# Two middle MLP groups of a decoder layer: pairs of units, with seven products of block sums in two of eight steps

## What is computed

```python
v = rms_norm(h, g_mlp[i])
h = h + jnp.square(jax.nn.relu(v @ w_mlp_up[i])) @ w_mlp_down[i]
h = h + jax.nn.sigmoid(h @ w_ple_gate[i]) * (p[i] @ w_ple_proj[i])
```

## Time and profile before

| | |
|---|---|
| median of three runs | 1570.44 us (1570.18 to 1570.52) |
| the profiled execution | 1570.37 us, of which the span of the profile is 1568.6 us |
| granted clock of TensorE | 0.998 of full speed |
| PE, DVE, ACT, POOL busy | 1560.0, 1073.4, 925.5, 147.8 us |
| MLP groups 1 and 2 | from 951 us of the span, 174 us each |

### The profile page before, as it was taken

How to read it: one execution, slowest core, us unless ns; L and a number is a source line. 1 busy time by engine, 2 the same in 40 slices (tenths; PEclk the granted TensorE clock), 3 DMA queues, 4 the chain that set the end, 5 groups by cost and what they waited for, 6 DMA issues and landing times.

```text
span 1568.6 us, 19800 instructions
## 1 busy us (share of the span) xinstructions
PE 1560.0 (99%) x7186; PEld 1287.6 (82%) x7186; DVE 1073.4 (68%) x1287; ACT 925.5 (59%) x1372; POOL 147.8 (9%) x247
## 2 busy tenths in 40 slices
PE   9999999999999999999999999999999999999998
PEld 8888887878878888888888888888888888888887
DVE  6679988768999958986655545565456555656665
ACT  6574466655454555767687544773467535777754
POOL 0222376443000000000000000000000000000000
PEclk9999999999999999999999999999999999999999
DMA  9766566656766668876656666666666666666663
GB/s 324 269 197 194 161 208 221 196 194 188 216 201 211 205 211 298 281 264 207 193 181 203 200 191 188 200 188 201 190 187 199 192 195 188 191 199 194 221 193 130
DMA packets 93764, 324.25 MB, mean 207 GB/s; under 512 B 10864, under 2 KB 14448, under 8 KB 93296
## 3 DMA queue, kind: packets, MB, share of 16 engines
q1 hardware_dynamic: 93536, 322.88, 66.0%
q10 hardware_dynamic: 144, 0.26, 0.1%
HBM read 312.62 MB, written 10.49 MB: 206 GB/s over the span
## 4 chain that ended last, share of the span: by engine, by line
PE 99%; ACT 0%; ACTq 0%; issue 0%; POOL 0%; DVE 0%; POOLq 0%
PE ps L427 32%; PE ps L429 31%; PE ps L428 31%; PE ps L731 0%; PE ps L734 0%; PE ps L988 0%; PE ps L987 0%; PE ps L989 0%; PE ps L737 0%; PE ps L815 0%; PE ps L840 0%; PE ps L891 0%; PE ps L715 0%; PE ps L902 0%; PE ps L802 0%; PE ps L746 0%
## 5 line engine op out<-in xcount | busy, mean ns | idle before, releaser
L410 DVE TENSOR_TENSOR sb<-sb,sb 128x1024 fp32r<-128x1024 f32 x552 | 676.8, 1231 | 407.6 <-ACT sb L403 402.3
L403 ACT ACTIVATE sb<-sb 128x1024 fp32r<-128x1024 f32 x552 | 581.9, 1057 | 522.2 <-PE ps L429 492.1
L427 PE MATMUL ps<-sb,sb 128*128 128x512 f32 (+1 forms) x2176 | 846.6, 389 | 0.0
L428 PE MATMUL ps<-sb,sb 128*128 128x512 f32 (+1 forms) x2176 | 843.8, 388 | 0.0
L429 PE MATMUL ps<-sb,sb 128*128 128x512 f32 (+1 forms) x2176 | 843.7, 388 | 0.0
L427 PEld LDWEIGHTS ps<-sb,sb 128*128 128x128 f32 x2176 | 408.4, 188 | 88.8 <-issue 4.2
L429 PEld LDWEIGHTS ps<-sb,sb 128*128 128x128 f32 x2176 | 408.4, 188 | 84.3
L428 PEld LDWEIGHTS ps<-sb,sb 128*128 128x128 f32 x2176 | 408.5, 188 | 83.1
L473 ACT ACTIVATE ps<-ps 32x256 f32<-32x256 f32 x464 | 162.8, 351 | 29.6 <-DVE ps L462 23.6
L1321 POOL TENSOR_TENSOR sb<-sb,sb 128x1 f32<-128x1 f32 x1 | 0.6, 560 | 1172.5 <-DVE sb L1990 1172.5
L499 POOL COPY sb<-sb 32x256 f32<-32x256 f32 (+1 forms) x112 | 76.0, 679 | 189.0 <-DVE sb L491 184.6
(11 more groups left out here) (238 smaller groups left out, 601.8 us busy)
## 6 DMA issues: line engine op xcount, KB each, us to landing
sb<-in_w_gate SPq DMA_DIRECT2D x128, 512.0 KB, 3.9
sb<-in_w_up SPq DMA_DIRECT2D x128, 512.0 KB, 3.9
sb<-in_w_down SPq DMA_DIRECT2D x128, 512.0 KB, 4.1
sb<-in_w_mix SPq DMA_DIRECT2D x56, 512.0 KB, 4.3
sb<-in_w_branch SPq DMA_DIRECT2D x32, 512.0 KB, 4.7
sb<-in_w_out SPq DMA_DIRECT2D x32, 512.0 KB, 3.8
sb<-in_w_pg SPq DMA_DIRECT2D x32, 512.0 KB, 4.0
gate_mem<-sb SPq DMA_DIRECT2D x16, 512.0 KB, 5.3
```

Source lines behind the costliest of these rows:

```text
L403: act.activation(whi[:, j % RING, :], raw[:, j % RING, :], ACT.Copy).then_inc(hi_done, 1)
L410: eng.tensor_tensor(wlo[:, j % RING, :], raw[:, j % RING, :], whi[:, j % RING, :].bitcast(F32), ALU.subtract).then_inc(lo_done, 1)
L427: pe.matmul(o, xh, w_h, start=first and k == 0, stop=False)
L428: pe.matmul(o, xh, w_l, start=False, stop=False)
```

## The change

Groups 1 and 2 leave `mlp_group` for a new body, four calls of `pair_of_units(g, p)` in each pass of the loop on each engine. A pair is two units (c = 0, 1) side by side, 16 tiles (i = 0 to 15). Steps j = 0 to 5 take unit 0's tile and then unit 1's tile of the same two k blocks; the last four tiles are (6, 0), (7, 0), (6, 1), (7, 1), so that unit 0 ends at tile 13 and unit 1 at tile 15. The pair's own sums lie in `acc` for an even pair and in `side` for an odd one.

In steps 2 and 5 (tiles 4 and 5, 10 and 11) the 2 x 2 x 2 block product of two token blocks, two k blocks and two units is made with seven products in place of eight. Three of the seven go into the pair's own banks and four into "temporaries", the banks of the other kind. For that DVE makes four sums of weight blocks (`t_raw`, in three operations) which ACT and DVE split into `t_high` and `t_low`, and `wlo` of the second tile is made only for its second half. The sums of token blocks (`up_raw`, `dn_raw`) are made once for v in group 0's seventh unit, and once a step for f in the second and third pair. At i = 12 ACT copies one temporary and DVE makes four linked sums of them into `extra` (the place of `t_raw`), which DVE adds to each unit's result. "Linked" means that DVE waits for the operation's own semaphore before the next.

The square of an up unit goes from DVE to ACT, behind the ReLU, which reads SBUF now (DVE has written main + extra there). Transposes go to SBUF (`pair_lane`), and of the sixteen block moves GpSimd makes eight and ACT eight. SP's loop covers groups 1 and 2 in the pair's order, and group 3's loads are written out.

```diff
+SEVEN = (2, 5)
+STEP_TILES = [2 * j for j in SEVEN]
+PAIR_ORDER = [(j, c) for j in range(TPU - 2) for c in range(2)] + [(j, c) for c in range(2) for j in (TPU - 2, TPU - 1)]
+UNIT_ENDS = [PAIR_ORDER.index((TPU - 1, c)) for c in range(2)]
+PAIR_STEPS = 48
...
+extra = at(t_at, [2, TT, CW])
+pair_lane = [scratch[:, 0, :], at(top, [TT * CW])]
...
+def pair_of_units(g, p):
+    up = p < PAIRS // 2
...
+    pe.wait_ge(temps_free, g * PAIRS + (p - PAIRS + 1))
+    if p == 0:
+        pe.wait_ge(grp_free, g * (4 * NCH) + (2 * G_FF - 2))
+    for i, (j, c) in enumerate(PAIR_ORDER):
+        u, jj = pair_tile(g, p, i)
...
+        if p == PAIRS // 2 and i in (0, TPU, TPU + TPU // 2):
+            pe.wait_ge(tp_lo, g * NCH + (TP_FF + {0: NCH - 2, TPU: NCH - 1}.get(i, NCH)))
...
+        if j in SEVEN:
+            if c:
+                continue
+            e = SEVEN.index(j)
+            if e == 0:
+                pe.wait_ge(grp_free, g * (4 * NCH) + (2 * G_FF + 4 * p))
...
+            pe.wait_ge(lo_done, u * TPU + (jj + 1))
+            three(temp_bank(p, 0), half(x_hi_, 0, 0), half(x_lo_, 0, 0), block(whi, s, 0), block(wlo, s, 0),
+                  first, last)
+            three(main_bank(p, 0, 0), half(x_hi_, 1, 0), half(x_lo_, 1, 0), block(whi, s, 1), block(wlo, s, 1),
+                  False, False).then_inc(tile_used, 1)
+            pe.wait_ge(lo_done, u * TPU + (jj + 2))
+            if up:
+                pe.wait_ge(up_sums_lo, len(SEVEN))
+            else:
+                pe.wait_ge(dn_sums_lo, g * len(SEVEN) + (e + 1 - len(SEVEN)))
+            three(main_bank(p, 1, 0), sh(4), sl(4), block(whi, s + 1, 1), block(wlo, s + 1, 1), False, False)\
+                .then_inc(tile_used, 1)
+            n = 2 * (len(SEVEN) * (p - PAIRS) + e)
+            pe.wait_ge(comb_lo, g * (2 * PAIRS * len(SEVEN)) + (n + 1))
+            three(temp_bank(p, 1), sh(1), sl(1), t_high[:, 0, :], t_low[:, 0, :], first, last)
+            three(temp_bank(p, 3), sh(3), sl(3), t_high[:, 1, :], t_low[:, 1, :], first, last)
+            pe.wait_ge(comb_lo, g * (2 * PAIRS * len(SEVEN)) + (n + 2))
+            three(temp_bank(p, 2), sh(2), sl(2), t_high[:, 2, :], t_low[:, 2, :], first, last)
+            three(main_bank(p, 0, 1), half(x_hi_, 1, 1), half(x_lo_, 1, 1), t_high[:, 3, :], t_low[:, 3, :],
+                  False, False).then_inc(seven_done, 1)
+            continue
...
             mlp_group(0, True, False)
             with pe.Fori(1, NFG - 1) as g:
-                mlp_group(g, False, False)
+    for p in range(PAIRS):
+        pair_of_units(g, p)
+pe.wait_ge(temps_free, (NFG - 2) * PAIRS + 1)
...
+def pair_of_units(g, p):
...
+    for i in range(2 * TPU):
+        u, jj = pair_tile(g, p, i)
+        t = i + AHEAD
+        if t - 1 in STEP_TILES:
+            e = STEP_TILES.index(t - 1)
+            s = (jj + AHEAD) % RING
+            act.wait_ge(raw_in[s], u * (16 * TPU // RING) + 16 * ((jj + AHEAD) // RING + 1))
+            act.wait_ge(tile_used, u * TPU + (jj + AHEAD - RING + 1))
+            act.activation(whi[:, s, C:2 * C], raw[:, s, C:2 * C], ACT.Copy).then_inc(hi_done, 1)
+            n = 2 * (len(SEVEN) * (p - PAIRS) + e)
+            if e:
+                act.wait_ge(seven_done, g * (PAIRS * len(SEVEN)) + (n // 2))
+            if p in (1, 2) and i == 2:
+                act_blocks(0, range(12, 16)).then_inc(tp_in, 1)
+            for b in range(2):
+                act.wait_ge(comb_raw, g * per + (n + b + 1))
+                act.activation(t_high[:, 2 * b:2 * b + 2, :], t_raw[:, 2 * b:2 * b + 2, :], ACT.Copy)\
+                    .then_inc(comb_hi, 1)
+        else:
+            split_hi(act, u, jj + AHEAD)
+        if i == 12:
+            act.wait_ge(seven_done, g * (PAIRS * len(SEVEN)) + len(SEVEN) * (p + 1 - PAIRS))
+            act.activation(extra[:, 0, 0, :], temp_bank(p, 0), ACT.Copy).then_inc(first_copied, 1)
+        def relu_square(c, q):
+            act.wait_ge(grp_free, g * (4 * NCH) + 2 * (G_FF + 2 * q + c + 1))
+            for tt in range(TT):
+                part = relu[c][:, tt * C:(tt + 1) * C]
+                ins = act.activation(part, part, ACT.Relu, scale=rstd[:, 1, tt:tt + 1])
+                ins.then_inc(relu_done, 1)
+            act.wait_ge(relu_done, g * (2 * NCH) + 2 * (2 * q + c + 1 - NCH))
+            act.activation(relu[c][:, :], relu[c][:, :], ACT.Square).then_inc(sg["sq_done"], 1)
+        if i == UNIT_ENDS[0] + 1 and p < 2:
+            relu_square(0, p)
+        if p in (1, 2):
+            n = 2 * (p - 1)
+            if i == 0:
+                relu_square(1, p - 1)
+            if i == 1:
+                act.wait_ge(strips_done, g * NCH + (TP_FF + n + 1))
+                act_blocks(0, range(8, 12))
+            if i == 5:
+                act.wait_ge(strips_done, g * NCH + (TP_FF + n + 2))
+                act_blocks(1, range(8, 12))
+            if i == 6:
+                act_blocks(1, range(12, 16)).then_inc(tp_in, 1)
+            if i in (3, 9):
+                n += i == 9
+                act.wait_ge(tp_in, g * NCH + (TP_FF + n + 1))
+                act.wait_ge(half_in, g * NCH + (n + 1 - NCH))
+                act.activation(f_hi[:, 4 * n:4 * n + 4, :].rearrange("p k t -> p (k t)"), relu[n % 2][:, :],
+                               ACT.Copy).then_inc(tp_hi, 1)
+            if i == (13 if p == 1 else 7):
+                act.wait_ge(dn_sums, g * len(SEVEN) + (p - len(SEVEN)))
+                act.activation(dn_high[:, p - 1, :, :], dn_raw[:, p - 1, :, :], ACT.Copy)\
+                    .then_inc(dn_sums_hi, 1)
...
+for g in range(1, NFG - 1):
+    for q in range(NCH):
+        gp.wait_ge(strips_done, g * NCH + (TP_FF + q + 1))
+        for i in range(8):
+            ins = gp.tensor_copy(*pair_block(q % 2, i))
+        ins.then_inc(half_in, 1)
...
+def pair_of_units(g, p, linked):
...
+    for i in range(2 * TPU):
+        u, jj = pair_tile(g, p, i)
+        t = i + AHEAD
+        s = (jj + AHEAD) % RING
+        if t - 1 in STEP_TILES:
+            e = STEP_TILES.index(t - 1)
+            v.wait_ge(hi_done, u * TPU + (jj + AHEAD + 1))
+            v.tensor_tensor(wlo[:, s, C:2 * C], raw[:, s, C:2 * C], whi[:, s, C:2 * C].bitcast(F32), ALU.subtract)\
+                .then_inc(lo_done, 1)
+            for b in range(2):
+                v.wait_ge(comb_hi, g * per + (2 * (len(SEVEN) * (p - PAIRS) + e) + b + 1))
+                v.tensor_tensor(t_low[:, 2 * b:2 * b + 2, :], t_raw[:, 2 * b:2 * b + 2, :],
+                                t_high[:, 2 * b:2 * b + 2, :].bitcast(F32), ALU.subtract).then_inc(comb_lo, 1)
+        elif t not in STEP_TILES:
+            split_lo(v, u, jj + AHEAD)
+        else:
+            v.wait_ge(hi_done, u * TPU + (jj + AHEAD + 1))
+            v.tensor_tensor(wlo[:, s, :], raw[:, s, :], whi[:, s, :].bitcast(F32), ALU.subtract)
+            if t != STEP_TILES[0]:
+                v.wait_ge(seven_done, g * (PAIRS * len(SEVEN)) + (len(SEVEN) * (p - PAIRS) + STEP_TILES.index(t)))
+            for k in range(2):
+                v.wait_ge(raw_in[s + k], u * (16 * TPU // RING) + 16 * ((jj + AHEAD) // RING + 1))
+            linked(v.tensor_tensor(t_raw[:, 0:2, :], raw[:, s + 1, :].rearrange("p (k n) -> p k n", k=2),
+                                   raw[:, s:s + 2, 0:C], ALU.subtract))
+            v.sem_inc(comb_raw, 1)
+            linked(v.tensor_tensor(t_raw[:, 2, :], t_raw[:, 1, :], raw[:, s, 0:C], ALU.add))
+            linked(v.tensor_tensor(t_raw[:, 3, :], raw[:, s, C:2 * C], t_raw[:, 2, :], ALU.subtract))
+            v.sem_inc(comb_raw, 1)
+            v.sem_inc(lo_done, 1)
+        def turn_unit(n):
+            v.wait_ge(sg["sq_done"], g * NCH + (n + 1))
...
+            ins.then_inc(strips_done, 1)
+        if i == 15 and p < 2:
+            turn_unit(2 * p)
+        if p in (1, 2):
+            if i == 3:
+                turn_unit(2 * p - 1)
+            if i in (4, 10):
+                n = 2 * (p - 1) + (i == 10)
+                v.wait_ge(tp_hi, g * NCH + (TP_FF + n + 1))
+                v.tensor_tensor(f_lo[:, 4 * n:4 * n + 4, :].rearrange("p k t -> p (k t)"), relu[n % 2][:, :],
+                                f_hi[:, 4 * n:4 * n + 4, :].rearrange("p k t -> p (k t)").bitcast(F32),
+                                ALU.subtract).then_inc(tp_lo, 1)
+            if i == (11 if p == 1 else 5):
+                x = relu[p % 2].rearrange("p (k t) -> p k t", k=4)
+                token_sums(linked, dn_raw[:, p - 1], x, TK * SEVEN[p - 1] % 4).then_inc(dn_sums, 1)
+            if i == (15 if p == 1 else 9):
+                v.wait_ge(dn_sums_hi, g * len(SEVEN) + (p - len(SEVEN)))
+                v.tensor_tensor(dn_low[:, p - 1, :, :], dn_raw[:, p - 1, :, :],
+                                dn_high[:, p - 1, :, :].bitcast(F32), ALU.subtract).then_inc(dn_sums_lo, 1)
+        if i == 12:
+            v.wait_ge(first_copied, g * PAIRS + (p + 1 - PAIRS))
```

(77 more changed lines are left out.)

76 lines of the change are left out of this document (74 added, 2 removed).

## The result

The changed kernel took 1581.93 us in the median of four executions (1577.07 to 1582.21), the kernel before 1570.43: a ratio of the means of 1.0066 (95% interval 1.0047 to 1.0086). It is slower, and that median lies above the range of the prediction (1563.5 to 1580). The profiled execution is the shortest of the four, 1577.07 us, with a span of 1575.3; by it the change costs 6.7 us. Nine more executions came with the experiments; all thirteen lie between 1576.9 and 1582.2, with a median of 1579.2, which is inside the range.

The account below looks back on a forecast made before the run. TensorE, busy 99%, was taken to bound the kernel, with DVE nearly full in the middle pairs. −10.9 + 1.75 + 2×(0.1+3.4+2.0+0.35) = +2.6 us gave 1573.0 us, range 1563.5 to 1580.

Parts of the forecast that it names:

- the removed work: In groups 1 and 2, 21 matmuls for 24 per seven-product step: 16×3×0.2266 = 10.9 us saved.
- the first wait: Third pair's tile 4: TensorE waits for DVE's weight sums, 3.4 us lost per group; 0.1 at the second pair's.
- the ledger: The prediction's priced, slot-by-slot account of DVE and ACT work in the pairs, set against TensorE's tile times.
- the entry: At the first pair TensorE waits for DVE's count after the first group's last residual sum: 1.75 us once, bounds 1.4 to 2.2.
- the second wait: Third pair's tile 12: TensorE waits for f_lo, 22.4 us of DVE work against 20.4, 2.0 us lost per group.
- GpSimd beside DVE: Block copies slow DVE's two-SBUF-input operations in the third pair: 0.35 us per group, bounds 0 and 1.0.
- The 1294 ns: Duration of six DVE low parts beside GpSimd copies, against 1231 in the mean; gave the price of 0.07 us each.
- 0.86 us: Length taken for one GpSimd copy beside a full DVE, 13.8/16.
- third rival: Third pair: DVE stands half a copy over some 12 operations, 5 us per group more, 1583; chance within a shared 0.24.
- DVE becomes the engine that sets both middle pairs: Weight-sum slots of second and third pair: late buffer returns cost 2 to 4 us more per group; 0.24 with third rival.
- not over 95: Sign expected in the changed kernel's profile: DVE busy over 95% in the second and third pair.
- the 11 to 14 announced: Sign expected in the changed kernel's profile: TensorE idle 11 to 14 us in all, at the entry and third pairs.

Follow-up runs that it names:

- both kernels without pauses: Changed kernel with seven products only in each group's first and last pair, 1565.72 us; or in all but the third, square behind tile 4's split, 1563.17 us.
- the kernel with the token sums sooner: Changed kernel with the third pair's token sums of f moved from slot 5 to 4, high part 7 to 5, low part 9 to 6: 1577.42 us.
- the kernel without copies: Changed kernel with square behind tile 4's split and earlier token sums, and GpSimd's eight block copies per unit left out: 1569.33 us, against 1572.49 with copies.
- the execution of 1579.2: Profiled execution of the changed kernel run again unaltered; that run took 1579.11 us in the median.
- the pause kernels: Kernel before the change, with TensorE made to wait at eight places for GpSimd fills: three fills 1597.83 us, six fills 1618.52 us.
- the kernel with both edits: Changed kernel with ACT's square of the second unit behind tile 4's split and the third pair's token sums made earlier: 1572.49 us, ratio to before 1.0015.
- the short pauses: Kernel before the change, with TensorE waiting at eight places for three GpSimd fills, about 2 us each: 1597.83 us.

## Why the prediction was wrong

**Right: the removed work.** 10.9 us; 48 records fewer, and both kernels without pauses come out at the removed matmuls × 0.2266 less the entry, within 0.1 and 0.4 us.

**Right: the first wait.** 3.4 us expected at the third pair's tile 4, 3.56 measured, 0.1 and 0.15 at the second pair's. The chain from DVE's sum to ACT's square to the split to the weight sums was as in the ledger: from the third pair's start at 1035.45 the sum was there after 6.9 us (6.3 expected), the split after 10.3 (9.9), the release after 14.5 (14.0). Moving the square took half of the pause away.

**Mis-sized: the entry.** 1.75 expected, bounds 1.4 and 2.2; 0.69 measured. TensorE went on at 950.83 while DVE's residual sum ran (950.51 to 951.74): this separate increment in DVE's queue did not wait for the operation ahead of it.

```profile
950.51 1.23 DVE L2075 TENSOR_TENSOR sb<-ps,sb 128x1024 f32<-128x1024 f32 x1 [0.41 <-PE ps L466]
950.83 0.49 PE L1037 MATMUL ps<-sb,sb 128*128 128x512 f32 x1 [0.42 <-DVEq L2241]
```

**Wrong: the second wait.** This is the step that failed: "from that release up to the low part of the last quarter of f ... 2.0 lost". The term is for the wrong wait. TensorE waits earlier, inside the step at tile 10, for the low part of the token sums, which slot 9 makes. I had priced those sums on DVE but never asked who waits for them. By the prediction's own prices DVE has 2.85+2.4+2.3+2.7+1.1+4.15+2.85+1.7 = 20.1 us from the release to that low part and TensorE 17.0: 3.1, not 2.0. The trace has 21.5 us for these slots (1050.07 to 1071.54), 1.4 over the prices: 1.5 more for the operations beside GpSimd's copies, 0.5 less for the token sums (1.05 us where no copy ran, 1.6 priced), the rest small waits. That the wait for f_lo existed underneath shows in the kernel with the token sums sooner: 1.8.

**Mis-sized: GpSimd beside DVE.** 0.35 a group taken, bounds 0 and 1.0; 1.6 by the kernel without copies, over four times my price, and 1.5 by the durations of one unit's copied operations in the changed kernel. Two readings of the earlier trace rows were wrong. The 1294 ns are a mean of unlike cases: of the six low parts, the two that directly followed another operation with two SBUF inputs took 1.42 and 1.41, the first and the two behind an operation that reads PSUM 1.18 to 1.23, one 1.30. DVE's full stretches of the third pair are all of the first kind (1.41 to 1.45, and 0.4 to 0.5 for the small ones of 0.28). And 0.86 us is not what a copy takes, nor did the sixteen at 106.30 run alone, since DVE worked beside them: of the 64 single copies in groups 1 and 2 of the changed kernel, the 36 that start beside an idle DVE or beside one of its operations with an input in PSUM take 0.4 us, and the 24 that start during a 128x1024 operation with both inputs in SBUF take 1.3 or 1.4, ending 0.2 to 0.3 behind it. So it is mostly GpSimd that stands for DVE, and DVE stands only for what is left of the copy, 0.2 of its next operation. That is the lock rule of the Trainium skill (SBUF — State Buffer, Who interferes with whom), by which the second of the two to start waits for the whole of the first; these traces agree with it. The third rival's 5 us came from the wrong length of a copy, not from the rule: with half of 0.39 us its twelve operations would give 2.3, by the same kind of estimate.

From 1049.95 to 1071.76 are 21.8 us where TensorE needs 17.0: 4.8 lost, of which 1.5 as slow matmuls and 3.3 as a pause. The 3.1 by the prices and the 1.4 by which DVE took longer make 4.5; the other 0.3 lie between the release and DVE's next operation and between L2218 and TensorE's start.

**Missing: the clock.** No term and no rival had it. In the profiled execution it costs nothing of its own: DVE's work sets the 4.8, and the slow matmuls lie inside it. Behind the last pause of a group it does: 1.2 us in the execution of 1579.2. With 0.69 + 2×(0.15+3.56+4.8) = 17.7 the profiled 1577.1 is explained; the 2 to 5 us above it, in 8 of 13 executions, are explained for the one profiled execution of 1579.2, but for 0.7 us ahead of group 1. For those at 1582 it is argued only: their clock was the lowest, and the pause kernels show up to 2.9 us for one pause.

**The rivals.** "DVE becomes the engine that sets both middle pairs" came nearest, 1577 to 1581, but by another mechanism and only in the third pair: not by bunched landings of loads (DVE waited for no load from 1034 to 1076). DVE was busy for 90 and 87% of the second and third pair, not over 95. TensorE's idle of 13.2 us lies within the 11 to 14 announced, but by luck: the entry took 1.3 less than priced, the second waits 1.4 more than priced with their share of the copies, and the slow matmuls are no idle time. The range ended at 1580 since I gave that case a fourth of the chance and no term for the clock; most executions fell inside it all the same.

## What to carry to other kernels

When the prices fill an engine off the critical path to 95%, list every semaphore that the critical engine waits for in that stretch and date each one, the small operands too; the earliest due one decides, and removing it only uncovers the next. A saving whose price is paid by another engine belongs where that engine has room: the same seven products brought 4.7 us when both crowded pairs were left out and 7.0 when only the third was and the square moved, and cost 9 (1579.2 against 1570.3) when none was. An experiment that undoes a change pair by pair finds this faster than repairs of single waits.

## What the runs showed of the hardware

A pause of 1.9 us idle was followed by a stretch at 1.2 GHz in six cases of eight, one of 3.7 us in eight of eight, pauses of up to 1.6 us idle in the kernel with both edits in none, and those of 2.9 to 3.2 us in the changed kernel's tile 10 in one of four. The stretch cost 1.2 to 2.9 us, and with the short pauses it began 0.7 to 1.6 us after the restart. The Trainium skill (TensorE: Matmul & The Clock Gate, HAM oscillation — how this bites in real kernels) tells of waits that send TensorE back to the lower clock; these traces agree. A GpSimd copy of 32x256 takes 0.39 us, and 1.3 when it starts during a DVE operation of 128x1024 with two SBUF inputs; DVE's next such operation then takes 1.41 to 1.45 instead of 1.22. In the kernel before, two sums with an input in PSUM (L1743, L1749) kept 1.22 and 1.21 beside copies, and the copies their 0.39.
